# A two-layer hybrid decoder step: swaps issued from another queue, key masks on another engine, fillers and a table load at other places

## The reference, cut to what matters

```python
h = _rmsnorm(x, p['norm_mix_pre'])
z = h @ p['w_in']
ya, s_wkv, s_shift = _rwkv7_branch(za, ...)   # a step per token: S = S*w - (S kk) b + v k
yb, s_ret = _retention_branch(zb, ...)        # rotary on q and k, chunkwise retention
m = sigmoid(ga) * (ya @ w_out_a) + sigmoid(gb) * (yb @ w_out_b)
x = x + _rmsnorm(m @ p['w_o'], ...)
x = x + _rmsnorm((silu(h @ w_gate) * (h @ w_up)) @ w_down, ...)
```

## Time and profile before

| | us |
|---|---|
| median of 3 runs (lowest, highest) | 1325.74 (1322.05, 1326.98) |
| the profiled execution | 1322.61 |
| its span, first to last instruction | 1320.8 |
| share of the span TensorE / VectorE / ScalarE / GpSimd busy | 95% / 66% / 41% / 8% |
| mean granted TensorE clock | 0.978 of full speed |

### The profile page before, as it was taken

How to read it: one execution, slowest core, us unless ns; L and a number is a source line. 1 busy time by engine, 2 the same in 40 slices (tenths; PEclk the granted TensorE clock), 3 DMA queues, 4 the chain that set the end, 5 groups by cost and what they waited for, 6 DMA issues and landing times.

```text
span 1320.8 us, 27667 instructions
## 1 busy us (share of the span) xinstructions
PE 1248.3 (95%) x11984; PEld 1174.5 (89%) x11984; DVE 866.6 (66%) x1460; ACT 545.4 (41%) x821; POOL 108.2 (8%) x124
## 2 busy tenths in 40 slices
PE   6999989999998999999989997999999989999996
PEld 5898877899997999999888986879989979999996
DVE  4887558777676566554477873578777656666533
ACT  5552334354445433343444533353434454333432
POOL 0004163000000000000000050720000000000000
PEclk9999989999998999999989999999999989999998
DMA  6433135544453544544423323264444534444541
GB/s 223 128 114 114 52 100 162 176 160 143 136 153 107 183 147 147 154 153 150 143 87 121 117 96 79 71 213 156 144 144 136 160 99 140 160 144 145 158 146 70
DMA packets 51177, 179.50 MB, mean 136 GB/s; under 512 B 6257, under 2 KB 7025, under 8 KB 49777
## 3 DMA queue, kind: packets, MB, share of 16 engines
q1 hardware_dynamic: 41904, 150.49, 36.3%
q10 hardware_dynamic: 9152, 27.25, 6.2%
HBM read 166.57 MB, written 8.53 MB: 133 GB/s over the span
## 4 chain that ended last, share of the span: by engine, by line
PE 83%; DVE 10%; issue 3%; ACT 3%; ACTq 1%; DMA 0%; SPq 0%; DVEq 0%
PE dense L1297 51%; PE core L1297 32%; DVE w_lo L841 2%; ACT w_hi L547 1%; DVE x L889 1%; DVE y_out L887 1%; ACTq L681 1%; DMA x<-x_t 0%; DVE s_gate L1104 0%; DVE s_st L1086 0%; DVE bonus L952 0%; DVE s_st L1087 0%; DVE u_exp L1031 0%; DVE y_a L1151 0%; DVE tmp L938 0%
## 5 line engine op out<-in xcount | busy, mean ns | idle before, releaser
L841 DVE TENSOR_TENSOR w_lo<-w_raw,w_hi 128x1024 fp32r<-128x1024 f32 x282 | 348.8, 1238 | 238.0 <-ACT w_hi L547 237.2
L547 ACT ACTIVATE w_hi<-w_raw 128x1024 fp32r<-128x1024 f32 x282 | 298.0, 1057 | 481.9 <-PE dense L1297 335.3
L1297 PE MATMUL dense<-h_hi,w_hi 128*128 128x320 f32 x1296 | 421.7, 325 | 26.1 <-DVE h_lo L845 14.5
L1297 PE MATMUL dense<-h_lo,w_hi 128*128 128x320 f32 x1296 | 407.1, 314 | 0.0
L1297 PE MATMUL dense<-h_hi,w_lo 128*128 128x320 f32 x1296 | 407.0, 314 | 0.0
L1297 PEld LDWEIGHTS dense<-h_hi,w_hi 128*128 128x128 f32 x1296 | 249.4, 192 | 43.6 <-issue 31.6
L1297 PEld LDWEIGHTS dense<-h_lo,w_hi 128*128 128x128 f32 x1296 | 249.9, 193 | 2.0 <-issue 0.2
L1297 PEld LDWEIGHTS dense<-h_hi,w_lo 128*128 128x128 f32 x1296 | 249.2, 192 | 0.0
L1297 PE MATMUL core<-h_hi,w_hi 128*128 128x320 f32 x416 | 129.8, 312 | 0.0
L1297 PE MATMUL core<-h_hi,w_lo 128*128 128x320 f32 x416 | 129.3, 311 | 0.0
L1297 PE MATMUL core<-h_lo,w_hi 128*128 128x320 f32 x416 | 129.3, 311 | 0.0
(11 more groups left out here) (293 smaller groups left out, 1974.9 us busy)
## 6 DMA issues: line engine op xcount, KB each, us to landing
w_raw<-wts SPq DMA_DIRECT2D x282, 512.0 KB, 3.5
ret_t<-ret_t ACTq DMA_DIRECT2D x16, 256.0 KB, 3.8
ret_s<-ret_t ACTq DMA_DIRECT2D x16, 256.0 KB, 2.4
ret_rest<-ret_d ACTq DMA_DIRECT2D x2, 1536.0 KB, 7.6
qk_rot<-qk_raw ACTq DMA_DIRECT2D x8, 320.0 KB, 6.5
dmask<-rconst ACTq DMA_DIRECT2D x2, 1152.0 KB, 7.1
s_st<-wkv_st ACTq DMA_DIRECT2D x2, 1024.0 KB, 6.0
wkv_s<-s_st ACTq DMA_DIRECT2D x2, 1024.0 KB, 4.4
```

The lines of the kernel that those rows point to most:

```text
L547: act.activation(w_hi[n % RING][:, :], w_raw[n % RING][:, :], ACT.Copy).then_inc(hi_ready.sem, 1)
L841: dve.tensor_tensor(w_lo[r][:, :], w_raw[r][:, :], w_hi[r][:, :].bitcast(F32), ALU.subtract).then_inc(low_made.sem, 1)
L1297: return pe.matmul(out, lhsT, rhs, start=start, stop=stop)
```

## The change

1. The cosine table and the four swaps are issued by SyncE, in its stream of weight loads, after the load of tile T_V+7 and so before that of T_V+8; it waits for VectorE's and for GpSimd's last job of the rounds.
2. The key products `kt` are copied out unmasked by ScalarE (two copies each) and masked in place by GpSimd (two multiplications each). GpSimd does kt0 and kt1 after b4, kt2 after p33, kt3 and kt4 last. TensorE waits for GpSimd's last job before the sequence.
3. The pieces move from the slots 4, 8, ..., 48 to 2, 5, 8, 12, 16, 20, 24, 28, 32, 37, 42, 48. The remainder of T_V+1 moves from slot 6 to slot 10.
4. Turn 3 moves from after ys of chunk 1 to after u of chunk 1, turn 5 from after ys of chunk 2 to after as3, turn 6 from after w of chunk 3 to after the sample's w.
5. The logarithm table is loaded after the first `mean`'s square and no longer at the first `var`. The store of the state is issued after the last exponential of the tail.

```diff
@@ -66,11 +66,12 @@
           "d22 tk4", "d23 e31", "e30 e32", "e14 vt1", "dt30 e33", "d30 dt31", "d31 dt32", "d32 dt33", "d33 vt2", "e40 e41",
           "dt14 e42", "tb1 vt3", "dt40 e43", "tb2 dt41", "tb3 dt42", "tb4 vt4", "dt43")
 THIRDS = ((0, 3), (3, 6), (6, 8))
-PIECE_AT = {4 * n + 4: (n // 3, THIRDS[n % 3]) for n in range(12)}
-LOW_AT = {6: 1, 18: 2, 30: 3, 42: 4}
+PIECE_AT = {at: (n // 3, THIRDS[n % 3]) for n, at in enumerate((2, 5, 8, 12, 16, 20, 24, 28, 32, 37, 42, 48))}
+LOW_AT = {10: 1, 18: 2, 30: 3, 42: 4}
 ROUND_BANKS = 6
 MASKS = ("xt0", "x1", "xt1", "x2", "xt2", "x3", "xt3", "x0", "p10", "p20", "p11", "p21", "p12", "p22", "p13", "p23", "xt4", "x4",
-         "p14", "k4", "b4", "p31", "p30", "p32", "p33", "p41", "p40", "p42", "p43")
+         "p14", "k4", "b4", "kt0", "kt1", "p31", "p30", "p32", "p33", "kt2", "p41", "p40", "p42",
+         "p43", "kt3", "kt4")
 
 
 def named(text):
@@ -83,12 +84,12 @@
 def on_act(job):
 
     name, lv, s = job
-    return name in ("vt", "tk", "tb") or (name == "e" and lv > 0) or (name == "m" and s in FLIP)
+    return name in ("vt", "kt", "tk", "tb") or (name == "e" and lv > 0) or (name == "m" and s in FLIP)
 
 
 JOBS = [named(t) for slot in ROUNDS for t in slot.split()]
 JOB_AT = {j: i + 1 for i, j in enumerate(JOBS)}
-PARTS = {"mt": ("xt", "mrb"), "kt": ("makt", "mrk"), "m": ("x", "m"), "mx": ("x",)}
+PARTS = {"mt": ("xt", "mrb"), "m": ("x", "m"), "mx": ("x",)}
 V_OPS = [(part, lv, s) for name, lv, s in JOBS if not on_act((name, lv, s)) for part in PARTS.get(name, (name,))]
 A_OPS = [j for j in JOBS if on_act(j)]
 P_OPS = [named(t) for t in MASKS]
@@ -100,8 +101,8 @@
        ("s0", SAMPLE), ("s1", SAMPLE), ("s2", SAMPLE), ("s3", SAMPLE)]
 V_FIRST = max(j for j, _ in PIECE_AT.values()) + 1
 FILL_AFTER = {("w", 0): [("turn", 0)], ("u", 0): [("turn", 1)], ("ys", 0): [("tile", 4)], ("w", 1): [("turn", 2)],
-              ("ys", 1): [("tile", 5), ("turn", 3)], ("w", 2): [("turn", 4)], ("ys", 2): [("tile", 6), ("turn", 5)],
-              ("w", 3): [("tile", 7), ("turn", 6)], ("u", 3): [("turn", 7)]}
+              ("u", 1): [("turn", 3)], ("ys", 1): [("tile", 5)], ("w", 2): [("turn", 4)], ("ys", 2): [("tile", 6)],
+              ("as3", SAMPLE): [("turn", 5)], ("w", 3): [("tile", 7)], ("w", SAMPLE): [("turn", 6)], ("u", 3): [("turn", 7)]}
 LOWS_AFTER = {("ys", 0): (5, 6), ("ys", 1): (7,), ("ys", 2): (8,), ("w", 3): (9,), ("y", SAMPLE): (10,)}
 
 TAIL = [("gate", 0), ("s", 0), ("mean", 0), ("mean", 1), ("s", 1), ("gate", 1), ("mean", 2), ("mean", 3), ("s", 2), ("s", 3),
@@ -446,8 +447,19 @@
                 sp.dma_start(x[:, cols], x_t[:, cols]).then_inc(x_loaded[i], 16)
                 if i in FIRST_WEIGHTS:
                     weights(FIRST_WEIGHTS.index(i))
+            def swaps(layer):
+
+                sp.wait_ge(*round_v(layer, len(V_OPS)))
+                sp.wait_ge(*round_p(layer, len(P_OPS)))
+                sp.dma_start(cos_sin[:, :], trig).then_inc(trig_loaded.sem, 16)
+                for i in range(4):
+                    to, of = 32 * i, 32 * (i ^ 1)
+                    sp.dma_start(qk_rot[to:to + 32, :], qk_raw[of:of + 32, :]).then_inc(qk_swapped.sem, 16)
+
             for n in range(len(FIRST_WEIGHTS), DEPTH * NT):
                 weights(n)
+                if n % NT == T_V + max(LOW_AT.values()) + RING:
+                    swaps(n // NT)
             for i, (lo, hi) in enumerate(X_GROUPS):
                 sp.wait_ge(*x_done(DEPTH - 1, i + 1))
                 sp.dma_start(y_t[:, lo * T:hi * T], x[:, lo * T:hi * T]).then_inc(y_stored, 16)
@@ -473,6 +485,11 @@
                     elif name == "x":
                         pool.wait_ge(*made(layer, op))
                         plus_one(x_sq, s).then_inc(round_p.sem, 1)
+                    elif name == "kt":
+                        pool.wait_ge(*made(layer, op))
+                        for t, o in ((makt, M_STRT), (mrk, M_INC)):
+                            ins = pool.tensor_tensor(pairs(t, s, C), pairs(t, s, C), mask(kind(s, o)), ALU.mult)
+                        ins.then_inc(round_p.sem, 1)
                     elif name == "p":
                         pool.wait_ge(*made(layer, ("m", 0, s)))
                         if lv >= 3:
@@ -668,17 +685,16 @@
                             continue
                         name, lv, s = job
                         act.wait_ge(*round_done(layer, JOB_AT[job]))
+                        if name == "kt":
+                            p128 = round_bank(job)[:, :].rearrange("p (m c) -> p m c", m=4)
+                            act.activation(pairs(makt, s, C), ar_of(p128, 0), ACT.Copy)
+                            act.activation(pairs(mrk, s, C), ar_of(p128, 1), ACT.Copy).then_inc(round_a.sem, 1)
+                            continue
                         to = {"vt": pairs(v_st, s, C), "m": pairs(m_sq, s, C), "e": pairs(e_sq, s, C),
                               "tk": pairs(tok, s, 128)[:, :, 0:C], "tb": pairs(tok, s, 128)[:, :, C:2 * C]}[name]
                         act.activation(to, round_bank(job)[:, 0:256].rearrange("p (m c) -> p m c", m=4), ACT.Copy).then_inc(round_a.sem, 1)
                     if i in PIECE_AT and PIECE_AT[i][1][1] == KT:
                         values(T_V + PIECE_AT[i][0])
-
-                act.wait_ge(*round_v(layer, len(V_OPS)))
-                act.dma_start(cos_sin[:, :], trig).then_inc(trig_loaded.sem, 16)
-                for i in range(4):
-                    to, of = 32 * i, 32 * (i ^ 1)
-                    act.dma_start(qk_rot[to:to + 32, :], qk_raw[of:of + 32, :]).then_inc(qk_swapped.sem, 16)
 
                 def turned_values(h):
 
@@ -741,9 +757,7 @@
                     elif what == "mean":
                         act.wait_ge(*cent_a(layer, i + 1))
                         act.activation(ch(sq_a, i), ch(y_a, i), ACT.Square).then_inc(squared_a.sem, 1)
-                    elif what == "s" and i == HP - 1:
-                        act.wait_ge(*seq_evac(layer, EVAC_AT["s3", SAMPLE]))
-                        act.dma_start(wkv_s[layer], s0_st[:, :]).then_inc(wkvs_stored.sem, 16)
+                        tables(LN_EXP)
                     elif what == "var":
                         tables(LN_EXP)
                         act.wait_ge(*var_a(layer, i + 1))
@@ -752,6 +766,8 @@
                 act.wait_ge(*log_a(layer, HP))
                 tables(LN_EXP)
                 act.activation(sq_a[:, :], sq_a[:, :], ACT.Exp, scale=-0.5).then_inc(root_a.sem, 1)
+                act.wait_ge(*seq_evac(layer, EVAC_AT["s3", SAMPLE]))
+                act.dma_start(wkv_s[layer], s0_st[:, :]).then_inc(wkvs_stored.sem, 16)
                 gates(T_GATE + 1, T_GATE + 3)
                 act.wait_ge(*wkvs_stored(layer, 1))
                 act.dma_start(ret0[1][:, :], ret_d[layer][:, 1024:4096]).then_inc(ret0_rest.sem, 16)
@@ -1007,9 +1023,6 @@
                     if name == "mt":
                         masked(xt, a_part, M_X1T)
                         masked(mrb, r_part, kind(s, M_INC))
-                    elif name == "kt":
-                        masked(makt, a_part, kind(s, M_STRT))
-                        masked(mrk, r_part, kind(s, M_INC))
                     elif name in ("m", "mx"):
                         masked(x_sq, p64, M_X1)
                         if name == "m":
@@ -1521,6 +1534,7 @@
                     plain(T_V, T_V)
                 need(round_v(layer, len(V_OPS)))
                 need(round_a(layer, len(A_OPS)))
+                need(round_p(layer, len(P_OPS)))
                 for name, c in SEQ:
                     w, u = (wu_s, wu_s) if c == SAMPLE else (w_st, u_st)
```

## The result

| | before | changed |
|---|---|---|
| median (lowest, highest) | 1325.91 (1322.05, 1326.98) us | 1307.39 (1305.50, 1308.13) us |
| ratio, with its 95% interval | | 0.9876 (0.9856 to 0.9895) |
| the profiled execution, its span | 1322.61, 1320.8 | 1308.13, 1306.4 |
| mean granted clock | 0.978 | 0.984 |

The account below looks back on a forecast made before the run. TensorE, busy 95% of the span, was taken as the bound. Terms 5.6+2.2+3.8+3.2-1.3-2.0+0 = 11.5 us gave 1311.1 from the profiled 1322.6, or 1314.2 from the median; forecast 1313, range 1305 to 1321.

Parts of the forecast that it names:

- cleaner than forecast: Rival, chance 0.11: no clock fall in the stages (4.8) and one issue gap less per layer (+4); gain 17, 1307.
- The swaps, 5.6: Sequence: with SyncE issuing them, TensorE's wait before turn 1 goes; 2.8 us per layer, 5.6 saved, bounds 4.0 to 5.8.
- The turns, 2.2: Sequence: moving turn 3 ends turn 4's wait of 1.25 us; 1.1 us per layer, 2.2 saved, bounds 0 to 3.4.
- The tail, 3.8: Tail: earlier logarithm table load ends TensorE's wait for the logarithm; 1.9 us per layer, 3.8 saved, bounds 2.4 to 3.8.
- The store priced at 0: Tail: state store and `ret_rest` go out later, but `ret_rest` is read over 20 us on, so cost 0.
- The clock, 3.2 of 4.8: Sequences and a tail: three half-speed hits of 1.6 us, 4.8; two thirds taken as saved, 3.2, bounds -1.6 to 4.8.
- the fall at 835 us: Layer 1: a clock fall with only gaps of 0.3 to 0.7 us before it, cited against saving the whole 4.8.
- GpSimd's end, -1.3: Sequence's end: GpSimd's last rotation can't come as much earlier, delaying ScalarE's tail work; 0.65 us lost per layer, bounds 0 to -3.
- The rounds, -2.0: Rounds: TensorE waits for ScalarE's copies behind the moved tile ends; 1.0 us lost per layer, bounds 0 to -6.
- the issue gaps, 0: Rounds: TensorE's stops look like late instructions; the moved pieces were taken as worth 0, from -4 to +4 us.

Follow-up runs that it names:

- the tails alone: Kernel before with only the logarithm table load moved after the first mean's square and the state store after the last exponential: 1316.48 us, 0.9949.
- the swaps alone: Kernel before with only the cosine table and the four swaps issued by SyncE instead of ScalarE: 1313.76 us, 0.9926.
- the four combinations: Changed kernel and three variants, ratios to kernel before: unedited 0.9876, key products back on VectorE 0.9878, pieces back 0.9912, both back 0.9868.
- the second trace: Changed kernel run once more, unedited, beside the kernel before: 1305.98 us, ratio 0.9876, profiled span 1302.4 us.
- the run with the table first: Changed kernel, but GpSimd multiplies the cosine table by the norm's root before it waits for the swaps: 1306.33 us, 0.9884.

## Why the prediction was right, step by step

The direction and the main reasons were right; the time fell at the lower part of the range, where the rival "cleaner than forecast" (1307) stood. Of that rival's two conditions the first nearly held (0.9 us at half speed left in the three stages in one trace, 3.4 in the other), the second in layer 0 only, as the issue gaps of layer 1 didn't shrink.

- **The swaps, 5.6.** Right. The waits before turn 1 (2.93 and 2.85 us) are gone, and nothing is late next. Alone the edit brings 9.8 us and taken back it costs 5.8, with the clock in both. SyncE's issues took 3.84 us and cost nothing, as forecast: the loads behind them go out at 168.2. By the rule weighed there (the Trainium skill, "Trainium Kernel Development and Optimization", section Key Constraints) only the issue time is saved, and the trace agrees: the swaps land 6.2 us after issue for 6.5 before (medians). They are issued some 0.7 us sooner, though, ahead of the end of the last tile, and GpSimd starts to scale the table 9.5 and 8.3 us after the rounds' end for 10.0 and 10.3.
- **The turns, 2.2.** Right in the mechanism, open in size. The waits before turn 4 are gone, and TensorE's waits in the sequence, that before turn 1 left aside, fall from 3.6 us to 2.8 and 2.6, near the 1.1 per layer forecast; a second wait of 0.73 us for `s_v` has come in. Taken back, the edit costs 2.6 us by the medians, with intervals that overlap, but the sequence of layer 0 shows 0.1 to 0.3 us of it only.
- **The tail, 3.8.** Right. Its waits are gone, and the tails alone lose 5.9 us with the clock.
- **The store priced at 0.** Wrong in the mechanism, and small in size. The prediction looked at who reads `ret_rest` and not at what ScalarE does while it waits to issue it. Before, the store was out at 227.56 and the load behind it at 232.00, with the table load, logarithms and the exponential of the earlier trace rows between; in the changed kernel the store goes out after the exponential, lands 8.1 us after issue (median; 4.4 before), and ScalarE stands 4.1 and 6.3 us for it. Behind it stand `ret_t` and so the retention core: 0.3 and 1.7 us of wait in one trace, 0.1 and 1.2 in the other, and one fall of the clock in one of them. The runs that take the wait away (the stores on GpSimd, `ret_rest` later) are no faster than the changed kernel, and the stretch behind the last tail is as long in nine of ten traces with the new place as before (431.8 to 433.9 us for 432.6). So 2 us is the most that can be claimed, and 0 can't be told from it.
- **The clock, 3.2 of 4.8.** Too small, by how it was counted. The prediction read 7 us at half speed per sequence and then priced one hit of 1.6 for each. The three stages (both sequences and the first tail) had 17.0 us at half speed before and have 0.9 in the first trace now, 3.4 in the second. What such a stretch costs, the swaps alone show in layer 0: the sequence is 5.7 us shorter, 2.9 of it the wait, so 6.8 us at half speed cost 2.8, or 0.4 each. By that, an estimate, the 16.1 or 13.6 us fewer of the two traces are worth 6.4 or 5.4. The third that was held back for the fall at 835 us was a guess: in the changed kernel's first trace there is none, in the second there is one of 3.4 us at 828.6.
- **GpSimd's end, -1.3.** Too large. It does set the start of the tail's ScalarE work (207.26, and the decay of the states waits for as3 no more, as forecast), but with that end sooner the tail of layer 0 was 0.6 us shorter at most and that of layer 1 no shorter.
- **The rounds, -2.0, and the issue gaps, 0.** The size was off: both rounds together are 0.2 us shorter in one trace and 1.8 in the other, where 2.0 more had been forecast. Of the waits for ScalarE behind the tile ends one is there (0.39 us for `m_sq` at slot 11, forecast 0.6), the others are not. The gaps went from 5.3 to 1.9 us in layer 0 and from 6.0 to 7.2 in layer 1, both within the range given; what they are was read rightly from the earlier trace rows. What the prediction missed are the shared ports: it put the ten masks on GpSimd at nothing because GpSimd had time, and by the four combinations they cost 5 to 6 us with the pieces at their old places and nothing with the new ones. That the new places avoid it is luck as far as the prediction goes, as it gave no reason of this kind for them.

In sum: 11.5 forecast, 14.4 between the profiled spans, and 18.4 with the second trace. In the first the clock is 3.2 more than forecast, GpSimd's end 0.7 to 1.3 less of a loss, the rounds 2.2 better; 3.3 were lost behind the tails, for which nothing had been set and of which the second trace has next to nothing, and of the turns' 2.2 up to 2 are not found in the stages. (In the chances, 0.65 + 0.11 should read 0.66 + 0.11.)

## What to carry to other kernels

When a store is followed on the same queue by a load that waits for it, look at the whole engine's wait and all that is queued behind, not only the reader of the load; here ScalarE stood 4 to 6 us per layer, though little of that reached the time. A wait of 3 us on TensorE was worth up to as much again by the clock that fell behind it (2.8 us in layer 0, 0.5 in layer 1, by the swaps alone), so count the half-speed time and not the falls. Before work is given to an idle GpSimd, look at which two-input operations VectorE has at that moment: a row of masks without a pause made one of 1.7 us take 5.2, with the pieces at one set of places and not at another. And take a second trace before a stage's loss of 2 or 3 us is explained.

## What the runs showed of the hardware

- VectorE's subtraction of two tensors in SBUF was held up for six GpSimd multiplications in a row (5.16 and 5.18 us for 1.69), while none of these was slowed. At the same slot of the changed kernel it waited for one mask only and then held up the next (1.69 us for 1.22 alone, and 1.73 for 0.75).
- An instruction packet of 16 KB behind a weight load of 512 KB came after it, 3.2 us after the load was issued. TensorE, out of instructions, went on 1.2 to 1.5 us after the packet's end, in six of six cases.
- The same program had a third issue gap of 2.32 us in one execution and of 0.49 in another, and a fall of the clock behind a wait of 2.02 us but none behind 1.51 in the other, nor behind 2.10 at the same place in the run with the table first.
- The 1 MB store took 8.1 us to land in the changed kernel (7.9 in its second trace), 4.4 in the kernel before, 6.2 with the tail alone changed, and 5.2 from GpSimd's queue, where it was issued 0.6 and 0.5 us earlier in the span than in the changed kernel (medians of two). Why it differs so much was not found.
